# First two tiles of the second block's input projection taken from undivided x, the shift as a bias, and one weight chunk's high part moved up in ScalarE's order

## The reference

```
x  = x + ga2 * ((silu(gate) * up) @ w_down)          # end of the first block
x1 = rmsnorm(x, g_final)                             # per token
h  = rmsnorm_2(x1, norm_g_2) * (1 + scale) + shift   # second block's norm and modulation
u  = h @ w_in_2                                      # 1024 -> 5120
cv, cg, cs, lx, ls = split(u)                        # 1024 columns each
v  = causal_depthwise_conv(cv * sigmoid(cg), dw_w)   # 31 taps
```

## Time and profile before

| | us |
|---|---|
| runs shown (median, lowest, highest) | 1058.04, 1057.92, 1058.24 |
| the profiled execution's own time | 1059.21 |
| its span, first to last instruction | 1057.4 |
| PE busy / DVE busy / POOL busy / ACT busy | 1037.7 / 628.8 / 472.2 / 421.4 |
| POOL's `w_lo` (line 589) | 368.8, x77, mean 4.79 |
| mean granted TensorE clock | 0.996 |

### The profile page before, as it was taken

The page is one execution under the profiler, slowest core; times in us unless marked ns, Lnnn a source line. Parts: engine busy times, 40 slices in busy tenths (PEclk is TensorE's granted clock), DMA queues, the critical chain, the costliest instruction groups (busy, mean ns, idle before and its releaser), DMA issues.

```text
span 1057.4 us, 14026 instructions
## 1 busy us (share of the span) xinstructions
PE 1037.7 (98%) x5222; PEld 838.3 (79%) x5222; DVE 628.8 (59%) x1223; ACT 421.4 (40%) x585; POOL 472.2 (45%) x176
## 2 busy tenths in 40 slices
PE   7999999999999999999999999999999999999997
PEld 5787796767878888888888888888887777888886
DVE  5367997786562432223337101679999999864322
ACT  4244325884241222212232222423435888362232
POOL 0034342692324443443533443347674766633340
PEclk9999999999999999999999999999999999999999
DMA  9984231140424335434374223223322222323212
GB/s 327 349 273 137 80 116 45 42 161 1 146 92 147 133 119 171 147 131 147 119 228 150 90 100 109 81 79 122 117 80 80 80 80 87 114 80 101 98 40 80
DMA packets 127250, 128.91 MB, mean 122 GB/s; under 512 B 3552, under 2 KB 125280, under 8 KB 127200
## 3 DMA queue, kind: packets, MB, share of 16 engines
q1 hardware_dynamic: 125952, 127.38, 36.9%
q10 hardware_dynamic: 1248, 0.86, 0.3%
HBM read 126.13 MB, written 2.10 MB: 121 GB/s over the span
## 4 chain that ended last, share of the span: by engine, by line
PE 53%; issue 33%; POOL 10%; DMA 1%; ACT 1%; SPq 1%; DVE 0%; POOLq 0%; DVEq 0%; ACTq 0%
PE bank L715 11%; PE bank L717 11%; PE bank L716 11%; POOL w_lo L589 10%; PE bank L1061 2%; PE bank L1032 2%; PE bank L904 2%; PE bank L1256 1%; PE bank L1257 1%; PE bank L1255 1%; DMA ada_stage<-in_w_ada 1%; PE bank L1213 1%; PE bank L922 1%; PE bank L740 1%; PE bank L741 1%
## 5 line engine op out<-in xcount | busy, mean ns | idle before, releaser
L589 POOL TENSOR_TENSOR w_lo<-w_stage,w_hi 128x2048 fp32r<-128x2048 f32 x77 | 368.8, 4790 | 489.2 <-ACT w_hi L1326 489.2
L715 PE MATMUL bank<-act_hi,w_hi 128*128 128x512 f32 x848 | 335.2, 395 | 0.5 <-POOL w_lo L589 0.4
L717 PE MATMUL bank<-act_hi,w_lo 128*128 128x512 f32 x848 | 330.1, 389 | 0.0
L716 PE MATMUL bank<-act_lo,w_hi 128*128 128x512 f32 x848 | 330.0, 389 | 0.0
L1326 ACT ACTIVATE w_hi<-w_stage 128x2048 fp32r<-128x2048 f32 x78 | 149.3, 1914 | 250.0 <-PE bank L717 236.2
L715 PEld LDWEIGHTS bank<-act_hi,w_hi 128*128 128x128 f32 x848 | 159.3, 188 | 39.2 <-issue 5.8
L717 PEld LDWEIGHTS bank<-act_hi,w_lo 128*128 128x128 f32 x848 | 159.1, 188 | 33.5
L716 PEld LDWEIGHTS bank<-act_lo,w_hi 128*128 128x128 f32 x848 | 159.3, 188 | 33.2 <-issue 1.4
L2167 DVE SCALAR_TENSOR_TENSOR bank<-v_pad,vcol,bank 128x512 f32<-128x512 f32 x208 | 138.2, 746 | 0.0
L2079 DVE TENSOR_TENSOR tmp<-bank,tmp 128x512 f32<-128x512 f32 x22 | 15.2, 692 | 157.0 <-PE bank L717 153.6
L715 PE MATMUL bank<-ff_hi,w_hi 128*128 128x512 f32 x176 | 69.7, 396 | 0.0
(11 more groups left out here) (317 smaller groups left out, 1533.7 us busy)
## 6 DMA issues: line engine op xcount, KB each, us to landing
w_stage<-in_w_in SPq DMA_DIRECT2D x29, 1024.0 KB, 5.1
w_stage<-in_w_gu SPq DMA_DIRECT2D x22, 1024.0 KB, 5.1
ada_stage<-in_w_ada SPq DMA_DIRECT2D x20, 1024.0 KB, 11.6
w_stage<-in_w_out SPq DMA_DIRECT2D x12, 1024.0 KB, 5.1
ada_stage<-in_mod_w SPq DMA_DIRECT2D x12, 1024.0 KB, 7.6
w_stage<-in_w_down SPq DMA_DIRECT2D x8, 1024.0 KB, 5.2
late_stage<-in_w_ada SPq DMA_DIRECT2D x4, 1024.0 KB, 9.2
w_stage<-in_pw_w SPq DMA_DIRECT2D x4, 1024.0 KB, 5.1
```

Source lines behind the costliest of these rows:

```text
L589: nc.gpsimd.tensor_tensor(w_lo[b][:], w_stage[b][:], w_hi[b][:].bitcast(F32), ALU.subtract).then_inc(s_lo, 1)
L715: pe.matmul(dst, wh, rhs_hi(k), start=(first and k == 0), stop=False)
L716: pe.matmul(dst, wh, rhs_lo(k), start=False, stop=False)
L717: mm = pe.matmul(dst, wl, rhs_hi(k), start=False, stop=(last and k == n_k - 1))
```

## The change

- PE makes chunk 49's two tiles (banks 0 and 1) from x times the factor per feature, not divided by the factor per token. ACT makes their high part (`act_hi`, a copy of `xT` with a scale), DVE the low part, behind each tile's squares. 12 products stand after the first halves of the square sums, 12 between the sums and the spreads, 24 after the spreads. The sums of x's squares go to bank 2, and the `keep_warm` products are gone here.
- DVE divides the two tiles afterwards (bank x factor per token), and ACT's sigmoid adds the bias, which is chunk 49's weights times the shift: eight 128 x 256 steps on DVE (`bias_rows`), two one-column products on PE before the last tile of `w_down`, one copy on DVE.
- Chunk 50's two tiles are taken abreast, from the divided parts, which are written over the undivided ones as these are used (`held`).
- ACT makes the high part of chunk 51 ahead of the seventh divided high part, no longer behind the sigmoids.
- The semaphores of the late modulation loads are gone; `s_ada` counts on. SP waits for the bias steps before it loads chunk 51.

```diff
@@ SP
-            stream(C_IN2, 4, [..., ...], first=1)
+            w_dma(C_IN2, w_cols(a["w_in_2"], 0, KD, D))
+            w_dma(C_IN2 + 1, w_cols(a["w_in_2"], 0, KD, 0))
+            sp.wait_ge(s_adaacc, len(ADA_ORD) + 1)
+            stream(C_IN2 + 2, 3, [..., ...], first=2)
@@ PE, square_sums
-                plain = 0 if gained else 6
+                plain = 2 if gained else 6
                 if gained:
                     pe.wait_ge(s_gsqused, KD - 2)
                     sums(7, tmp[2], True, False)
+                    pe.wait_ge(s_res, 2 * KD - 1)
...
                 if meanwhile:
                     meanwhile()
+                    if gained:
+                        spread(6, 7)
                     if spreads_back:
                         spread(4, 5)
                     return
                 keep_warm(WARM_COLUMNS, idle)
-                if gained:
-                    spread(6, 7)
                 spread(4, 5)
@@ PE, after the last but one tile of w_down
+                        if (m2, g, m) == (KD // 2 - 1, 2, 0):
+                            pe.wait_ge(s_adaacc, len(ADA_ORD) + 1)
+                            for c in range(2):
+                                mm = pe.matmul(bank[7][:, NCOL + c:NCOL + c + 1], ada2_acc[:, c * P:(c + 1) * P], ones[:, 0:1],
+                                               start=True, stop=True)
+                            mm.then_inc(s_adamm, 1)
+            def undivided(ks):
+                for k in ks:
+                    pe.wait_ge(s_rawlo, k + 1)
+                    for dst, cols, ready in ((bank[0][:], low, s_i2acc), (bank[1][:], high, s_wused)):
+                        wh, wl = w_hi[b0][:, k, cols], w_lo[b0][:, k, cols]
+                        pe.matmul(dst, wh, act_hi[:, k, :], start=(k == 0), stop=False)
+                        pe.matmul(dst, wh, act_lo[:, k, :], start=False, stop=False)
+                        mm = pe.matmul(dst, wl, act_hi[:, k, :], start=False, stop=(k == KD - 1))
...
+            square_sums(gained=True, before=first_undivided, meanwhile=lambda: undivided((2, 3)))
+            undivided(range(4, KD))
             pe.wait_ge(s_res, 2 * KD)
             pe.wait_ge(s_lo, C_IN2 + 2)
-            abreast(third, 2, range(KD // 4))
-            abreast(two, 2, range(KD // 2, KD))
-            abreast(third, 2, range(KD // 4, KD))
-            tile(bank[3][:], b1, high, KD, hi, lo).then_inc(s_wused, 1)
+            abreast([(bank[2][:], b1, low, s_i2acc), (bank[3][:], b1, high, s_wused)], 2)
@@ ACT, act_hi_parts(..., held=True)
                 for k in range(KD):
+                    if held and k == KD - 2:
+                        hi_part(C_IN2 + 2, C_IN2 % 2, (C_IN2 + 2) // 2)
+                    if held and k < KD - 1:
+                        act.wait_ge(s_rawused, k + 1)
+                    elif held:
+                        act.wait_ge(s_wused, C_IN2 + 1)
                     act.wait_ge(s_u, KD * j + k + 1)
@@ ACT, behind the squares of each tile
+            def undivided_high(k):
+                if k == 0:
+                    act.wait_ge(s_mod, 11)
+                nc.scalar.activation(act_hi[:, k, :], xT[:, k, :], ACT.Copy, scale=scale1[:, 0, k:k + 1]).then_inc(s_rawhi, 1)
@@ ACT, the first two sigmoids
+                            if j == 0:
+                                act.wait_ge(s_div, m + 1)
+                                act.wait_ge(s_mod, 12)
+                                nc.scalar.activation(tmp[m][:], tmp[m][:], ACT.Sigmoid, bias=first_bias[:, m:m + 1]).then_inc(s_sig, 1)
+                                continue
...
-                    hi_part(j * 2 + (C_IN2 + q + 2), (C_IN2 + q) % 2, j + (C_IN2 + q + 2) // 2)
+                    if j or q:
+                        hi_part(j * 2 + (C_IN2 + q + 2), (C_IN2 + q) % 2, j + (C_IN2 + q + 2) // 2)
@@ DVE, residual
+                    if gained and k == KD - 2:
+                        bias_rows()
+                    if gained and k == KD - 1:
+                        dve.wait_ge(s_adamm, len(ADA_ORD) + 1)
+                        V.tensor_copy(first_bias[:], bank[7][:, NCOL:NCOL + 2]).then_inc(s_mod, 1)
                     if k >= 1:
                         add_squares(k - 1, gained)
+                    if gained and k >= 1:
+                        dve.wait_ge(s_rawhi, k)
+                        V.scalar_tensor_tensor(act_lo[:, k - 1, :], xT[:, k - 1, :], scale1[:, 0, k - 1:k],
+                                               act_hi[:, k - 1, :].bitcast(F32), ALU.mult, ALU.subtract).then_inc(s_rawlo, 1)
@@ DVE, behind normed
             normed(0, SH3, bank[6], (5, 7))
+            link(V.tensor_copy(rstd[:], bank[6][:]))
+            for m in range(2):
+                dve.wait_ge((s_i2acc, s_wused)[m], (1, C_IN2 + 1)[m])
+                V.tensor_tensor(tmp[m][:], bank[m][:], rstd[:], ALU.mult).then_inc(s_div, 1)
```

More of the change, by code:

```diff
@@ L198, in build @@
         nothing, _ = fixed("nothing", [P, 8], at=at_expinv)
+        first_bias, _ = fixed("first_bias", [P, 2], at=at_expinv + 64)
         ckv_ss, _ = fixed("ckv_ss", [P, 3, TT])
@@ L313, in build @@
         s_adaloop = sem("ada_loop_loaded")
-        s_late_ada = [sem(f"late_ada_loaded{b}") for b in range(len(ADA_LATE))]
         s_adastep = sem("ada_step")
@@ L337, in build @@
         s_sdg = sem("gained_deviation_ready")
+        s_rawhi = sem("undivided_hi_ready")
+        s_rawlo = sem("undivided_lo_ready")
+        s_rawused = sem("undivided_parts_used")
+        s_div = sem("first_tiles_divided")
         s_rc = sem("inverse_columns_ready")
@@ L548, in late_dma @@
                 sp.dma_start(late_stage[b][:], w.rearrange("(p t) c -> p t c", t=KD)[:, :, j * NCOL:(j + 1) * NCOL]).then_inc(
-                    s_late_ada[b], 16)
+                    s_ada[b], 16)
             for n in range(12):
@@ L561, in _ @@
                     late_dma(2 * n - 2)
-            stream(C_IN2, 4, [lambda j: w_cols(a["w_in_2"], 0, KD, j * NCOL + (D - NCOL)),
-                              lambda j: w_cols(a["w_in_2"], 0, KD, j * NCOL - NCOL)], first=1)
+            w_dma(C_IN2, w_cols(a["w_in_2"], 0, KD, D))
+            w_dma(C_IN2 + 1, w_cols(a["w_in_2"], 0, KD, 0))
+            sp.wait_ge(s_adaacc, len(ADA_ORD) + 1)
+            stream(C_IN2 + 2, 3, [lambda j: w_cols(a["w_in_2"], 0, KD, j * NCOL + (D - NCOL)),
+                                  lambda j: w_cols(a["w_in_2"], 0, KD, j * NCOL - NCOL)], first=2)
             for g in range(2):
@@ L1183, in _, with first_undivided @@
                             late_products(b)
-            square_sums(gained=True)
+                        if (m2, g, m) == (KD // 2 - 1, 2, 0):
[4 more added lines that the diff above has]
+                            mm.then_inc(s_adamm, 1)
+            b0, b1 = C_IN2 % 2, (C_IN2 + 1) % 2
+            def undivided(ks):
[6 more added lines that the diff above has]
+                        mm = pe.matmul(dst, wl, act_hi[:, k, :], start=False, stop=(k == KD - 1))
+                        if k == KD - 1:
+                            mm.then_inc(ready, 1)
+                    if k < KD - 1:
+                        mm.then_inc(s_rawused, 1)
+            def first_undivided():
+                pe.wait_ge(s_lo, C_IN2 + 1)
+                pe.wait_ge(s_res, 2 * KD - 2)
+                undivided((0, 1))
+            square_sums(gained=True, before=first_undivided, meanwhile=lambda: undivided((2, 3)))
+            undivided(range(4, KD))
             pe.wait_ge(s_res, 2 * KD)
[L1187 to L1190, removed]
             pe.wait_ge(s_lo, C_IN2 + 2)
-            abreast(third, 2, range(KD // 4))
-            abreast(two, 2, range(KD // 2, KD))
-            abreast(third, 2, range(KD // 4, KD))
-            tile(bank[3][:], b1, high, KD, hi, lo).then_inc(s_wused, 1)
+            abreast([(bank[2][:], b1, low, s_i2acc), (bank[3][:], b1, high, s_wused)], 2)
             with pe.Fori(1, KD // 2) as j:
@@ L1373, in squares, with act_hi_parts @@
                 act.wait_ge(s_col, j)
-                nc.scalar.activation(cols[:, 4, :], first_of_block(bank[0 if gains else 6]), ACT.Sqrt, bias=eps[:, 0:1], scale=1.0 / D).then_inc(s_sd, 1)
+                nc.scalar.activation(cols[:, 4, :], first_of_block(bank[2 if gains else 6]), ACT.Sqrt, bias=eps[:, 0:1], scale=1.0 / D).then_inc(s_sd, 1)
             splits = [0]
-            def act_hi_parts(shift, banks):
+            def act_hi_parts(shift, banks, held=False):
                 j = splits[0]
@@ L1577, in _ @@
             act.wait_ge(s_gains, 1)
-            squares(down_tile, gains=True)
+            def undivided_high(k):
+                if k == 0:
+                    act.wait_ge(s_mod, 11)
+                nc.scalar.activation(act_hi[:, k, :], xT[:, k, :], ACT.Copy, scale=scale1[:, 0, k:k + 1]).then_inc(s_rawhi, 1)
+            squares(down_tile, gains=True, behind=undivided_high)
             after(C_DOWN + 11)
             act.wait_ge(s_mod, 6)
-            act_hi_parts(SH3, (5, 7))
```

(13 more changed lines are left out.)

## The result

1065.18 us (median of 4, 1065.07 to 1065.28) against 1057.98 (4 runs, 1057.89 to 1058.24): ratio 1.0068, 95% interval 1.0055 to 1.0081. The change makes the kernel 7.2 us slower, outside the range given; it is rival D, whose price was 1065.

What follows compares the result with a forecast made beforehand. PE, busy 98%, was taken as the bound. A 2.8 us lead at the seam, cut to 1.0 by DVE and POOL blocking each other, gave 1057.1 against 1058.04; range 1055.2 to 1060.9.

Steps and rivals of the forecast that it cites:

- rival D: Behind the seam, POOL is let in between DVE's steps wherever it waits; 7 us slower, 1065; chance 0.08.
- Seam: Between the blocks, chunk 51 starts at 694.8, not 697.62: PE leads by 2.8 us, all added work hidden.
- (1): Line 2162's pair near 742 us meets chunk 56's low part and one POOL addition; DVE 4.1 us late.
- (2): From tile 6's v_pad: chunk 59 blocks the short convolution until 781.7, the next pair runs free; DVE 0.95 us early.
- it needs 4.65 from there: The first short convolution, once chunk 59's low part ends at 781.7, finishes undisturbed in 4.65 us.
- (3): Near 810 us DVE is first by 0.35, chunk 62's low part stands until 817.4, PE keeps 1.0 of 2.8.
- a rule read off one row: A POOL low part arriving during DVE's run stands until that run ends, as chunk 62's did: 9.60 us, not 4.6.
- five microseconds to win back: Up to the pair near 791 us, DVE loses 4.1 us and wins back 5.05.

Runs made afterwards that it cites:

- Experiment 3: Changed kernel with POOL's low part of chunk 60 held until the first short convolution is done, chunk 56's left free: 1060.91 us.
- experiment 4: Changed kernel with POOL's low parts of chunks 60 and 62 held until the short convolution's first and second pair are done: 1057.09 us.
- experiments 5: Changed kernel with only POOL's low part of chunk 56 held until DVE's first pair of line 2233 is done: 1055.24 us.
- 11: Changed kernel with chunk 56's low part held, and chunk 62's held until the first of the second short convolution's six steps is done: 1055.21 us.
- 12: Changed kernel with chunk 56's low part held, and chunk 62's held until the third of the second short convolution's six steps: 1055.49 us.
- experiment 9: Kernel before, with the first step of the second block's convolution computed five times more on DVE: 1068.08 us.

## Why the prediction was wrong

- **Seam: right.** 694.8 forecast, 694.82 found; the convolution starts at 698.5 (698.7 forecast), the slack of 0.70 at tile 3's `v_pad` is gone. No wait of PE between 668 and 694.
- **(1): right.** The pair ends at 747.5 on the old scale (747.6 forecast), with one addition of POOL's between its steps.
- **(2): right up to chunk 59's low part**, which ends at 780.30, 781.6 on the old scale (781.7 forecast). **The step that failed stands right behind it: "it needs 4.65 from there".** That held only if chunk 60's low part, due in the middle, would stand as chunk 62's does in the earlier trace rows. It was let in; the six steps took 8.41. DVE was not 0.95 early but late by 4.6, then met chunk 61's low part (5.76 for the pair that was to take 1.3) and was 7.6 late. Experiment 3 takes this one block away and gets back 4.3 us; with the later meeting of chunk 62 excluded too (experiment 4), 8.1.
- **(3) would have failed too**: in experiment 3 DVE was first by 0.36 and POOL was let in. The earlier trace rows didn't show that case: there the low part comes at 813.23, behind the two TENSOR_SCALAR steps and into the first of the six, and stands through seven more steps (not ten, as the prediction counts); in (3) it comes ahead of the TENSOR_SCALAR steps. With both orders forced (experiment 4) the forecast's sum gives 1057.1 and so does the chip, 1057.09. So no term was mis-sized by much; a rule read off one row was applied to two places where it didn't hold.
- **Rival D** had the mechanism, both blocks and the total (1065). Its chance of 0.08 came from weighing against the page. The Trainium skill (SBUF — State Buffer, "Who interferes with whom") has issue order decide who blocks, and at 783.28 and 794.16 the trace agrees (waits of 0.26 and 0.33, behind the one running step); at 809.25 in experiment 3 POOL was passed over by one step (0.76) and then let in; at 813.23, and in experiments 5, 11 and 12, the trace doesn't agree. D placed PE's wait at tile 3's products; it was at tile 2's, and a third of the loss, 2.3 us, was lower clock, which no step of the prediction had. The total agreed partly by luck.

The trace of the kernel before held the row that speaks against (2). Its first short convolution, POOL's chunk 59 below it:

```profile
776.60 9.45 DVE L2194 SCALAR_TENSOR_TENSOR tmp<-l_pad,vcol,tmp 128x512 f32<-128x512 f32 x6
...
777.78 5.06 POOL L589 TENSOR_TENSOR w_lo<-w_stage,w_hi 128x2048 fp32r<-128x2048 f32 x1
```

The same six steps, and a low part let into them after 0.45 us. The earlier trace rows have another: 5.03 is 4.62 and a wait of 0.4, between the two steps of line 2162. The prediction used that block only as five microseconds to win back, and took the rule for who is let in from the other short convolution.

## What to carry to other kernels

When a change moves one engine against another that shares a port with it, write down the order of the two queues before and after, and look at every meeting, not at the first; here 2.8 us of lead cost 7.2, and one wait at the head of the chain turned them into a gain of 2.8. A wait that pins the good order costs nothing when the held instruction has slack (7.76 us of idleness before it here, no PE wait behind). And look at the clock behind an idle TensorE: 3.35 us of idleness cost 1.6 more, 6.7 us cost 2.7 more, while the waits of 1.9 to 2.3 us in experiments 3 and 4 had a granted clock of 1.00 behind them.

## What was unexpected of the hardware

- **Who is let in.** A low part of POOL that comes while DVE runs two-tensor steps back to back either waits for one step (0.45 at 777.78 before, 0.26 at 783.28 after, about as much at 786.34 in experiment 9) or for all of them (the instruction then takes 9.60 in the earlier trace rows, 9.61, 8.90 and 7.57 in experiments 5, 11 and 12, instead of 4.62). Among the runs of six steps, every case of the first kind was the first short convolution and a run that had begun blocked by POOL (its two TENSOR_SCALAR steps took 2.23, 4.06 and 4.08 us instead of 0.99); every case of the second kind was a later one that had begun free. But a run needn't begin blocked: the pairs of line 2233 at 793.90 and, in experiment 9, of line 2162 at 796.97 began free, and chunk 61's low part was let in between their two steps (4.94 and 4.95 for 4.62, 5.76 for both pairs). What decides stays open; which step of the run it is, and the moment within a step, are excluded.
- **Between a run of line 2280 and the TENSOR_SCALAR steps behind it** POOL was let in, although that run had begun free (experiment 3, a wait of 0.76); one case.
- **The clock.** PE idle for 3.35 us came back at full pace, and only 0.7 us later the granted clock fell to the lower level, for some 3.4 us; kept busy with products that nobody reads it didn't fall, and the kernel was 1.65 us faster.
